# A split-float32 attention kernel: the fifth product of each score chunk on 64 rows of the array, two chunks at a time

## What is computed

```python
scores = (jnp.einsum('bqhd,bkhd->bhqk', qn_b, k_nope)
          + jnp.einsum('bqhd,bkd->bhqk', qr_b, k_rope)).astype(jnp.float32) * scale
q_idx = i * Q_BLOCK + jnp.arange(Q_BLOCK)
mask = key_idx[None, :] <= q_idx[:, None]
scores = jnp.where(mask[None, None], scores, -jnp.inf)
p = jax.nn.softmax(scores, axis=-1).astype(v.dtype)
return jnp.einsum('bhqk,bkhd->bqhd', p, v)
```

## Time and profile before

| | us |
|---|---|
| median of 3 runs (2578.85 to 2579.63) | 2579.59 |
| the profiled execution | 2580.04 |
| its span in the trace | 2578.2 |
| PE busy in it | 2528.8 |
| DVE busy | 1716.1 |
| ACT busy | 883.3 |
| POOL busy | 683.8 |

### The profile page before, as it was taken

One profiled execution on the slowest core, in us unless ns is written; L12 is line 12 of the kernel. 1 busy time (PEld: TensorE's weight loads), 2 busy tenths in 40 slices (PEclk: granted clock), 3 DMA queues, 4 the chain that ended last, 5 costly groups with the idle time before them and its releaser, 6 DMA issues. The chain is left out here.

```text
span 2578.2 us, 30788 instructions
## 1 busy us (share of the span) xinstructions
PE 2528.8 (98%) x12058; PEld 2090.3 (81%) x12058; DVE 1716.1 (67%) x2031; ACT 883.3 (34%) x1749; POOL 683.8 (27%) x617
## 2 busy tenths in 40 slices
PE   5999999999999999999999999999999999999998
PEld 4788888888888888888788888888888788888887
DVE  5688797989889898766466666766667522223343
ACT  4542111111111111233456565566566521111221
POOL 1322111111111111132143343344344210423322
PEclk8999999999999999999999999999999999999999
DMA  8023321313213121289824224224223263757532
GB/s 312 36 92 115 91 58 59 91 49 91 57 59 91 50 84 57 67 269 307 277 101 135 82 72 135 82 72 135 82 70 108 85 233 130 237 199 233 189 133 82
DMA packets 192141, 316.48 MB, mean 123 GB/s; under 512 B 14234, under 2 KB 106462, under 8 KB 181373
## 3 DMA queue, kind: packets, MB, share of 16 engines
q1 hardware_dynamic: 181984, 288.93, 34.4%
q0 software_dynamic: 5120, 16.78, 2.0%
q10 hardware_dynamic: 4892, 8.81, 0.9%
HBM read 207.52 MB, written 106.95 MB: 122 GB/s over the span
## 5 line engine op out<-in xcount | busy, mean ns | idle before, releaser
L52 PE MATMUL ps_proj<-h_hi,w_hi 128*128 128x512 f32 x1664 | 654.4, 393 | 6.7 <-DVE h_lo L975 6.0
L54 PE MATMUL ps_proj<-h_hi,w_lo 128*128 128x512 f32 x1664 | 648.5, 390 | 0.0
L53 PE MATMUL ps_proj<-h_lo,w_hi 128*128 128x512 f32 x1664 | 648.4, 390 | 0.0
L1089 DVE SCALAR_TENSOR_TENSOR acc<-u,taps_t,acc 128x2048 f32<-128x2048 f32 x240 | 629.0, 2621 | 8.5
L868 POOL TENSOR_TENSOR w_lo<-raw,w_hi 128x1024 fp32r<-128x1024 f32 x50 | 170.4, 3408 | 790.4 <-ACT w_hi L567 790.4
L52 PEld LDWEIGHTS ps_proj<-h_hi,w_hi 128*128 128x128 f32 x1664 | 312.9, 188 | 73.1 <-DVE h_lo L975 6.8
L53 PEld LDWEIGHTS ps_proj<-h_lo,w_hi 128*128 128x128 f32 x1664 | 313.1, 188 | 65.3 <-issue 1.4
L54 PEld LDWEIGHTS ps_proj<-h_hi,w_lo 128*128 128x128 f32 x1664 | 312.9, 188 | 65.3
L2094 POOL TENSOR_SCALAR prob<-prob,rinv 128x512 f32<-128x512 f32 (+2 forms) x320 | 199.3, 639 | 347.9 <-DVE rinv L1977 344.7
L2038 DVE TENSOR_TENSOR pt_lo<-ps_t,pt_hi 128x512 fp32r<-128x512 f32 (+1 forms) x320 | 192.8, 607 | 75.5 <-ACT pt_hi L1955 71.8
L2021 DVE TENSOR_REDUCE nmax<-ps_ring 128x1 f32<-128x512 f32 (+3 forms) x288 | 176.4, 623 | 94.7 <-PE ps_ring L1821 76.8
(11 more groups left out here) (289 smaller groups left out, 4054.2 us busy)
## 6 DMA issues: line engine op xcount, KB each, us to landing
qlat<-qlat_dram SPq DMA_DIRECT2D x32, 1024.0 KB, 7.7
raw<-in_w_in_dram SPq DMA_DIRECT2D x50, 512.0 KB, 6.4
under_h<-in_w_ada_dram SPq DMA_DIRECT2D x8, 1024.0 KB, 14.8
ga_dram<-lat SPq DMA_DIRECT2D x8, 1024.0 KB, 5.0
gb_dram<-lat SPq DMA_DIRECT2D x8, 1024.0 KB, 5.2
agate_dram<-lat SPq DMA_DIRECT2D x8, 1024.0 KB, 5.0
conv_dram<-acc SPq DMA_DIRECT2D x8, 1024.0 KB, 3.9
v_dram<-v_st SPq DMA_DIRECT2D x4, 2048.0 KB, 8.7
```

The source lines that it names most:

```text
L52: pe.matmul(out, wh, xh, start=first, stop=False)
L53: pe.matmul(out, wh, xl, start=False, stop=False)
L54: return pe.matmul(out, wl, xh, start=False, stop=last)
L1089: dve.scalar_tensor_tensor(acc[:], u[:, n:n + S], tap(n), acc[:], ALU.mult, ALU.add).then_inc(conv_tap if n < TAPS - 1 else conv_done, 1)
```

## The change

The fifth product of a chunk (L1821) contracts over 64 rows instead of 128: the high half of the rotary query by the low half of the rotary key. The product of the two low halves is left out. `kr_lo2` becomes half as wide: rows 0 to 63 hold the even key chunks, rows 64 to 127 the odd ones. A second tile `qr2` holds the query's high half on rows 64 to 127, written by one more ACT copy per chunk of the rotary query. The fifth product of an even chunk is held back until the first four of the odd chunk after it (and its mask) have been issued; then both are issued one after the other, the even one on rows 0 to 63, the odd one on rows 64 to 127, into two banks. An even chunk that is the block's last has its fifth product alone. The mask now comes before the fifth product.

```diff
--- before.py
+++ after.py
@@ -526,7 +526,9 @@
                 store_second(1)
                 store_values(1)
                 queries(3)
-                rotary_key(1, k.kr_lo2)
+                key_low = k.kr_dram[1].rearrange("r (c a n) -> r a c n", a=2, n=TC)
+                for a in range(2):
+                    next_load(k.kr_lo2[a * ROPE:(a + 1) * ROPE].bitcast(F32).rearrange("r (c n) -> r c n", n=TC), key_low[:, a])
                 store_second(2)
                 store_values(2)
                 store_second(3)
@@ -811,6 +813,7 @@
                         act.wait_ge(f.rope_done, c - 1)
                     act.activation(k.ra[c % 2][:], k.qb_first[ROPE:P, chunk(c)], ACT.Copy).then_inc(f.rope_shift, 1)
                     act.wait_ge(f.rope_sum, c + 1)
+                    act.activation(k.qr2[ROPE:P, chunk(c)], k.ra[c % 2][:], ACT.Copy)
                     act.activation(k.qr[0:ROPE, chunk(c)], k.ra[c % 2][:], ACT.Copy).then_inc(f.rope_hi, 1)
 
                 for kind, n in UNITS:
@@ -1818,11 +1821,17 @@
                         pe.matmul(out, qn_lo[:, q], kn_hi[:, ks], start=False, stop=False)
 
                         pe.matmul(out, qr[:, q], k.kr_hi2[:, ks], start=False, stop=False)
-                        mm = pe.matmul(out, qr[:, q], k.kr_lo2[:, ks], start=False, stop=(c < g))
                         if c == g:
-
-                            mm = pe.matmul(out[:, b * P:(b + 1) * P], k.ident16[:], k.mask[:], start=False, stop=True)
-                        mm.then_inc(scores_mm, 1)
+                            pe.matmul(out[:, b * P:(b + 1) * P], k.ident16[:], k.mask[:], start=False, stop=False)
+                        key_lo = slice(c // 2 * TC, c // 2 * TC + width)
+                        if c % 2 == 0:
+                            even_out, even_lo = out, key_lo
+                        if c % 2 or c == g:
+                            pe.matmul(even_out, qr[0:ROPE, q], k.kr_lo2[0:ROPE, even_lo], start=False,
+                                      stop=True).then_inc(scores_mm, 1)
+                        if c % 2:
+                            pe.matmul(out, k.qr2[ROPE:P, q], k.kr_lo2[ROPE:P, key_lo], start=False,
+                                      stop=True).then_inc(scores_mm, 1)
 
                 def turn(at, n):
                     g, j = TILES[n]
@@ -1914,6 +1923,7 @@
                         elif kind == "RH":
                             act.wait_ge(rope_sum, at.per(NC_, NC_ + n + 1))
                             s = slice(n * TC, (n + 1) * TC)
+                            act.activation(k.qr2[ROPE:P, s], ra[n % 2][:], ACT.Copy)
                             act.activation(qr[0:ROPE, s], ra[n % 2][:], ACT.Copy).then_inc(rope_hi, 1)
                         elif kind == "RS":
 
@@ -2472,7 +2482,7 @@
             k.wh, k.wl = sb("head_w_h", [P, LT, 3 * P], F32R), sb("head_w_l", [P, LT, 3 * P], F32R)
             k.prob = sb("prob", [P, PROB], F32)
             k.v_hi, k.v_lo = sb("v_hi", [P, S // P, VD], F32R), sb("v_lo", [P, S // P, VD], F32R)
-            k.kr_hi2, k.kr_lo2 = sb("kr_hi2", [P, S], F32R), sb("kr_lo2", [P, S], F32R)
+            k.kr_hi2, k.kr_lo2 = sb("kr_hi2", [P, S], F32R), sb("kr_lo2", [P, S // 2], F32R)
             k.pt_hi = [sb(f"pt_hi{i}", [P, TC], F32R) for i in range(PT_SLOTS)]
             k.pt_lo = [sb(f"pt_lo{i}", [P, TC], F32R) for i in range(PT_SLOTS)]
             k.bg = sb("bg", [P, TC], F32)
@@ -2481,9 +2491,13 @@
             k.kn_hi, k.kn_lo = sb("kn_hi", [P, S], F32R), sb("kn_lo", [P, S], F32R)
             k.qr = sb("qr", [P, S], F32R)
             k.ra = [sb(f"rope_a{i}", [ROPE, TC], F32) for i in range(2)]
+            sb("qr2_rest", [P, S - 2 * TC], F32)
             k.rb = sb("rope_rows", [P, TC], F32)
             k.nmax, k.rsum = (sb(n, [P, 16, NC_], F32) for n in ("nmax", "rsum"))
             k.nbias, k.rinv = (sb(n, [P, 16], F32) for n in ("nbias", "rinv"))
+        with ExitStack() as qctx:
+            qctx.enter_context(nc.sbuf_tensor("to_qr2", [P, ATTN_HELD + PROB + 10 * S + 3 * TC], F32))
+            k.qr2 = qctx.enter_context(nc.sbuf_tensor("qr2", [P, S], F32R))
         with ExitStack() as vctx:
             sb = lambda n, shape, d: vctx.enter_context(nc.sbuf_tensor(n, shape, d))
             sb("values_begun", [P, ATTN_HELD], F32)
@@ -2492,7 +2506,7 @@
             sb("to_v_st", [P, PROB - 4 * LT * TC - S - V_ST], F32)
             k.v_st = [None, None, sb("v_st2", [P, H, 4, VD], F32)]
             k.v_st[0] = sb("v_st0", [P, H, 4, VD], F32)
-            sb("kr_held", [P, 2 * S], F32)
+            sb("kr_held", [P, S + S // 2], F32)
             k.v_st[1] = sb("v_st1", [P, H, 4, VD], F32)
         with ExitStack() as octx:
             k.o_v = octx.enter_context(nc.sbuf_tensor("o_v", [P, KT, TC], F32))
```

## The result

| us | before | after |
|---|---|---|
| median of 4 runs each | 2579.61 (2578.85 to 2581.01) | 2668.53 (2668.09 to 2670.11) |
| the profiled execution | 2580.04 | 2670.11 |

The ratio is 1.0345 [1.0327, 1.0363]: 88.9 us slower. The prediction was 2647, in the range 2580 to 2680.

A forecast was written before the change was run, and what follows sets the result against it. PE, busy in 736.5 of attention's 742 us, was taken as the bound. Mode changes 47.4, ring 16.8 and copies 3.6 sum to 67.8 us on 2580.0, giving 2647.8; forecast median 2647, range 2580 to 2680.

The forecast's parts named there:

- Part 1: Fifth products in attention: leaving the 128-row mode costs about 0.18 us a change, a pair saves 0.12; +47.4 us.
- the place at the start: The trace's one change of mode, 68-row product then 31-row loads: upper bound 0.22 us a change.
- the marks the forecast gave: Timeline signs: load 0.3 late, pair 0.1 apart, next 128-row product over 0.3 later, ring wait from 9 to 20 us.
- Part 2: Ring of banks between attention blocks: the even chunk is counted late, one more maximum before the exponentials; +16.8 us.
- The fourth place: A fourth ring place a head, not waiting before: between 0 and 0.6 us there, 0.3 taken.
- The mask's new place: Mask ahead of the fifth product: the same work in another place, counted as nothing.
- Part 3: Extra ACT copy per 512 rotary queries, 32 in all: five tails and the front's end; +3.6 us (0.6 to 10).
- B: Rival, chance 0.08: no price for the change of mode, but the ring takes the gain back; some 2584 to 2594.
- C: Rival, chance 0.12: faster, a mode change costs under 0.05 us and the ring holds nothing; 2555 to 2569.
- E: Rival, chance 0.05: neither drain nor overlap in the fifth products, only the ring and the copies; 2600.
- D: Rival, chance 0.07: a pair's two products run one after the other, with drains; 2663 to 2686.
- A: The main case, as forecast, chance 0.68: its own range 2595 to 2686, highest with 0.22 and 0.17 a change.

The follow-up runs named there:

- the late copy: The changed kernel with the tails' extra ACT copies moved behind the copy DVE waits for and behind the tile's pt_hi: 2649.28 us, ratio 1.0272.
- the order alone: The changed kernel with the held-back fifth products on all 128 rows and without the extra ACT copies: 2605.04 us, ratio 1.0097.
- 64 rows without pairs: The kernel before with each of the 320 fifth products on rows 0 to 63 in its old place: 2688.61 us, ratio 1.0421.
- both late copies: The changed kernel, and its version with 64 rows for full pairs only, each with the tails' copies moved behind pt_hi: 2649.28 and 2597.09 us.
- the full pairs on 128 rows: The kernel before with the order changed for full pairs only, on 128 rows, without the copy: 2584.84 us, ratio 1.0023.
- the reordered tail: The kernel before with the rotary copy (RH) behind the second tile of the tail's step, not between the two: 2575.53 us, ratio 0.9987.

## Why the prediction was right, and where it wasn't

**Part 1, the mode: the mechanism right, the agreement of the sums partly luck.** A change costs 0.20, not 0.18: the place at the start, 0.22, was a better measure than the mean with the lower bound. The change behind a mask costs 0.15, not 0.13. The change back before a transposition costs some 0.05 less than the others, which the prediction did not separate. And a full pair saves 0.23, not 0.12: both products start together. So a full pair costs 0.17 (forecast 0.24), a masked pair 0.15 (0.19), a single 0.31 (0.31): 40 us against 47.4. That the two kernels lie 45.9 apart comes for the most part from 5 to 6 us of lower granted clock after, which has no term in the prediction. Of the marks the forecast gave, the late load (0.32), the late next product and the ring's longer wait were there; "the two products start 0.1 apart" was wrong.

The load at 1645.97 waited until 0.08 before the end of L1823, and the exit the same, so the trace agrees with "Mode switching requires drain" (the Trainium skill, TensorEngine Tiling (Array Packing), Key Properties), on both sides of the excursion. It also agrees with the packing rule that the prediction set beside its own 0.12 (the Trainium skill, TensorE: Matmul & The Clock Gate, Packing small matmuls): two row tiles started 0.00 to 0.01 us apart.

**Part 2, the ring: the mechanism right, its size too small.** Forecast 16.8, measured 24.8. The fourth place, for which half was taken, waits as long as the others, and the three others lose 0.79 - 0.30 = 0.49 each, not 0.6; that gives 18. The mask's new place, which the prediction put at nothing, gives some 3. The rest is open. That DVE's bunched maxima cost nothing through pt_lo in groups 1 and 2 held: 5.2 us of waiting in place of 4.9.

**Part 3, the copy: the term that was mis-sized.** Forecast 3.6 with bounds 0.6 to 10, measured 19.2. The step that failed is "in the five tails where PE already waits for pt_lo it adds 0.54 to 1.1; elsewhere it is covered by the projections". It counted places where PE waited, at most one a tail, and miscounted them: four of the five waits of the earlier trace rows stand in tails, the fifth in the last head, which has none. In fact the steps of a tail run as a chain from ACT's pt_hi over DVE to the next step, and each of the 24 steps with the copy between its two tiles carries the 0.64; 3.4 us of lower clock come on top. The row that shows the chain was in the trace of before, DVE's 0.58 for pt_hi ahead of L2038.

**The rivals.** B, C and E fall with the price of a change: the load of L1830 isn't hidden. D falls with the common start of the pair and with the 0.23 us that a full pair loses when both products stand on the same rows. C's condition, a change under 0.05 us, is missed by a factor of four; and even the cheapest part of the change, full pairs with a late copy, stays 18.3 us slower than before.

**What made 2647 too low by 21 us:** 15.6 in the copy and 8.0 in the order, less 1.5 in the mode, and 1.0 that the three parts together are more than the whole. The result lies in the range because the range was wide: its upper end came from rivals (half of D, and A's dearer changes of mode), not from the copy and the order, which were what was too small.

## To carry to other kernels

Half-height products pay only if an excursion from the 128-row mode saves more than its two changes: here 0.40 us at 512 columns, against 0.23 saved by a pair; a single one saves nothing. Two full pairs in one excursion would gain 0.06 by these numbers, and the run with all products at the block's end lost it many times over in waits. Holding back the last product of a chunk delays whoever reads that chunk, and a ring of buffers makes that PE's wait. Before calling a small copy covered, follow what stands behind it on its own engine (here pt_hi), and count the steps in which that engine's output is waited for, not the places where the bounding engine waits. And before two numbers that agree are taken as proof, read the same term off the trace: here 5 to 6 us of clock stood in for a price that was 7 us too high.

## What was not expected of the hardware

**The clock fell in places where before kept it.** Before is granted 1.00 on the mean of attention. After reads 0.90 in the first 52 us and 0.97, 0.93 and 0.97 in the three later windows of 52 us shown above. The short windows show one such place: in 1617 to 1621 PE worked 3.02 of 4 us (it waited 1.0 for qn_lo at the start of a head), and in the next 4 us it was granted 0.50, which is the lower level, 1.2 GHz: busy throughout, it ran 12 matmuls there, against 17 in the window before with its gap. The three later stretches lose 52 x (0.03 + 0.07 + 0.03) = 7 us of clock. With the late copy the waits for qn_lo are 0.3 at most and the program reads 1.00 from 1340 to 2100 us, and 0.90 before it as after does. So of the 19.3 us that the late copy gives back, up to 7 are clock and 8.7 are waits of PE (11.1 - 4.5 for pt_lo, 2.9 - 0.9 for qn_lo, 0.1 for `prob`); the rest was not traced. The fourteen traces divide in two. The seven kernels with an extra copy ahead of pt_hi in the tails have waits of 1.4 us for pt_lo and of 1.0 for qn_lo, and all seven lose clock in attention beyond its first 15 us. The other seven (before, the order alone, 64 rows without pairs, both late copies, the full pairs on 128 rows and the reordered tail) have waits for pt_lo of at most 1.1 and for qn_lo of at most 0.4, and lose none there. But not every long wait is followed by a fall, and no run varies the waits alone; so that they bring the falls is likely, not shown.

**Two row tiles start at the same time.** Both loads and both products of a pair of 64 rows carry the same start, and the pair of 512 columns takes 0.43 us to the next load (1645.97 to 1646.40), as one such product does (1640.68 to 1641.11 in the kernel without pairs).
